# Moving the score step of the next mLSTM job ahead of the transposes of the present one, in a one-core decoder layer

## The reference, cut to what matters

```
s   = (q @ k^T) * exp(Dm - m_t)                    # scores of the chunk
num = w_inter * (q @ C) + s @ v                    # old state, and values
den = w_inter * (q . n) + sum(s)
h   = num / max(|den|, exp(-m_t))
C   = a_prev * C + (k * weight)^T @ v              # state carried to the next chunk
hn  = (h - mean(h)) * rsqrt(var(h) + eps) * g      # norm of each head
y_b = sigmoid(o) * hn
```

## Time and profile before

| | |
|---|---|
| median of 3 runs | 2973.88 us (2971.07 to 2974.53) |
| profiled execution, its own time | 2971.51 us |
| its span | 2969.8 us |
| PE busy | 2812.3 us, 95% |
| DVE busy | 1464.4 us, 49% |
| ACT busy | 865.9 us, 29% |
| POOL busy | 131.0 us, 4% |
| mean granted clock of TensorE | 0.973 |

### The profile page before, as it was taken

How to read it: one execution, slowest core, us unless ns; L and a number is a source line. 1 busy time by engine, 2 the same in 40 slices (tenths; PEclk the granted TensorE clock), 3 DMA queues, 4 the chain that set the end, 5 groups by cost and what they waited for, 6 DMA issues and landing times. The chain is left out here.

```text
span 2969.8 us, 44214 instructions
## 1 busy us (share of the span) xinstructions
PE 2812.3 (95%) x17401; PEld 2719.9 (92%) x17401; DVE 1464.4 (49%) x3023; ACT 865.9 (29%) x1396; POOL 131.0 (4%) x190
## 2 busy tenths in 40 slices
PE   5899999999999898999998998999899999999997
PEld 3799999999999888988988988998799999999996
DVE  4655455445443736436445534644764344343446
ACT  5422222222212422342333234234431111111114
POOL 2100000000002100000000000000200000000002
PEclk7899999999999999999999999999899999999998
DMA  7133223222210205212111220221111111111111
GB/s 232 44 99 99 97 87 99 88 96 79 76 43 15 58 25 152 72 43 77 54 61 33 88 71 29 91 72 43 50 43 43 42 42 42 42 42 42 42 43 61
DMA packets 168691, 197.48 MB, mean 66 GB/s; under 512 B 7896, under 2 KB 157172, under 8 KB 168517
## 3 DMA queue, kind: packets, MB, share of 16 engines
q1 hardware_dynamic: 168130, 195.62, 20.7%
q10 hardware_dynamic: 342, 0.15, 0.0%
q0 software_dynamic: 96, 0.00, 0.0%
HBM read 176.84 MB, written 18.91 MB: 66 GB/s over the span
## 5 line engine op out<-in xcount | busy, mean ns | idle before, releaser
L522 DVE SCALAR_TENSOR_TENSOR xT<-ps,gate_p,xT 128x384 f32<-128x384 f32 (+1 forms) x624 | 348.1, 570 | 116.3 <-PE ps L802 97.7
L908 PE MATMUL ps<-hhi,mw_hi 128*128 128x384 f32 (+1 forms) x1152 | 393.8, 342 | 8.7 <-DVE mw_lo L1702 7.6
L739 DVE TENSOR_TENSOR hf<-st,ps 128x384 f32<-128x384 f32 x132 | 70.2, 532 | 642.5 <-PE ps L823 640.4
L909 PE MATMUL ps<-hlo,mw_hi 128*128 128x384 f32 (+1 forms) x1152 | 381.3, 331 | 0.0
L910 PE MATMUL ps<-hhi,mw_lo 128*128 128x384 f32 (+1 forms) x1152 | 380.9, 331 | 0.0
L821 PE MATMUL ps<-hhi,wa_hi 128*128 128x384 f32 (+1 forms) x1056 | 350.2, 332 | 17.4 <-DVE wa_lo L729 14.5
L822 PE MATMUL ps<-hlo,wa_hi 128*128 128x384 f32 (+1 forms) x1056 | 347.9, 329 | 0.0
L823 PE MATMUL ps<-hhi,wa_lo 128*128 128x384 f32 (+1 forms) x1056 | 347.5, 329 | 0.0
L821 PE MATMUL ps<-hhi,wb_hi 128*128 128x384 f32 (+1 forms) x1056 | 346.1, 328 | 0.0
L823 PE MATMUL ps<-hhi,wb_lo 128*128 128x384 f32 (+1 forms) x1056 | 346.0, 328 | 0.0
L822 PE MATMUL ps<-hlo,wb_hi 128*128 128x384 f32 (+1 forms) x1056 | 345.9, 328 | 0.0
(11 more groups left out here) (296 smaller groups left out, 5087.1 us busy)
## 6 DMA issues: line engine op xcount, KB each, us to landing
ada_raw<-in_w_ada SPq DMA_DIRECT2D x36, 1024.0 KB, 5.1
mw_raw<-in_w_in SPq DMA_DIRECT2D x32, 1024.0 KB, 5.7
wa_raw<-in_w_ffn_in SPq DMA_DIRECT2D x22, 1024.0 KB, 5.1
wb_raw<-in_w_ffn_in SPq DMA_DIRECT2D x22, 1024.0 KB, 5.2
wo_raw<-in_w_ffn_out SPq DMA_DIRECT2D x22, 1024.0 KB, 5.0
ada_raw<-in_w_ada_final SPq DMA_DIRECT2D x8, 1024.0 KB, 5.5
cs<-in_state_mlstm_C SPq DMA_DIRECT2D x32, 256.0 KB, 5.5
out_C_sample<-cs SPq DMA_DIRECT2D x32, 256.0 KB, 2.4
```

What stands on the lines that cost most here:

```text
L522: ins = dve.scalar_tensor_tensor(out=xT[:, m, t0:t0 + wp], in0=ps[:, bank, 0:wp], scalar=gate_p[:, m:m + 1], in1=xT[:, m, t0:t0 + wp], op0 ...
L739: dve.tensor_tensor(M["hf"][:, n, 0:w], M["st"][:, n, 0:w], ps[:, up_bank("b", b, i, n), 0:w], ALU.mult).then_inc(C["hidden"].sem, 1)
L908: pe.matmul(out, wh, xh, start=(j == 0), stop=False)
L909: pe.matmul(out, wh, xl, start=False, stop=False)
```

## The change

The list of stages is put in another order, and the waits on PE follow it:

```diff
-            for gap in range(3 * NJ):
-                EVENTS.append(("stage", gap // 3, gap % 3))
+            stages = [(0, 0)]
+            for p in range(NJ):
+                stages += [(p, 1)] + [(p + 1, 0)] * (p + 1 < NJ) + [(p, 2)]
+            for gap, (p, stage) in enumerate(stages):
+                EVENTS.append(("stage", p, stage))
                 while unit < ((gap + 1) * 8 + 8) // 9:
@@ pair() of PE, in front of the matmuls of a pair
-                        pe.wait_ge(*K["st_done"](h * NJ + p + 1))
+                        pe.wait_ge(*K["st_done"](h * NJ + p + 2))
@@ stage0() of PE, in front of the transposes of k
-                            if p:
-                                pe.wait_ge(*K["h_kept"](h * NJ + p))
-                            else:
+                            if p > 1:
+                                pe.wait_ge(*K["h_kept"](h * NJ + p - 1))
+                            if p and place(p - 1)[0]:
+                                pe.wait_ge(*K["inter_done"](h * 8 + place(p - 1)[1] + 1))
+                            if not p:
                                 pe.wait_ge(*K["kw_done"](h * NJ + 1))
@@ in front of the scores
-                            if p <= PAIRS:
-                                pe.wait_ge(*K["seq_upd"](h * PAIRS + p))
+                            if 2 <= p <= PAIRS + 1:
+                                pe.wait_ge(*K["seq_upd"](h * PAIRS + p - 1))
@@ stage1() of PE
                             pe.wait_ge(*K["kw_done"](h * NJ + c + 2))
+                            if p:
+                                pe.wait_ge(*K["h_kept"](h * NJ + p))
@@ in front of scores times values
                             pe.wait_ge(*K["b5_read"](h * NJ + p))
+                            if p <= PAIRS:
+                                pe.wait_ge(*K["seq_upd"](h * PAIRS + p))
@@ stage2() of PE, in front of the transposes of num
                         if chunk:
                             pe.wait_ge(*K["inter_done"](h * 8 + c + 1))
+                        if p + 1 < NJ and place(p + 1)[0]:
+                            pe.wait_ge(*K["kw_done"](h * NJ + place(p + 1)[1] + 2))
                         else:
                             pe.wait_ge(*K["h_kept"](h * NJ + p))
```

## The result

The changed kernel takes 2948.43 us (median of 4 runs, 2947.67 to 2953.17), the kernel before 2974.19 us beside it. The ratio is 0.9919, with a 95% interval of 0.9902 to 0.9936: 25.8 us faster, where 20 were forecast (2954, range 2943 to 2966). The profiled execution took 2947.84 us, 23.7 less than the one of before. By the times alone the forecast's own stretch, 2949 to 2959, is missed by half a microsecond; the wider range holds it.

The account below looks back on a forecast made before the run. PE was taken to bound the kernel, busy 2812.3 of 2969.8 us, so only its waits could be won. Terms -16.3 + 5.1 - 1.4 - 7.4 = -20.0 us, clock 0, gave 2954 us, range 2943 to 2966.

Parts of the forecast that it names:

- (a): Stage 1 to stage 2 in jobs 0 to 7: a second unit removes DVE waits except job 8's, -16.3 us.
- (b): Job 2 to 3: scores' wait for the pair goes, new waits of 3.3 us a head come; +5.1 us.
- (c): Job 5 to 6: transposes of k stop waiting for ACT's copy, those of num wait for kw; -1.4 us.
- (d): End of the head: job 8's exponential moves before unit 21, so the last mix comes earlier; -7.4 us in all.
- (e): Pairs of jobs 0 and 1: scores ready in time with a margin of 0.35 us, cost 0.
- (f): Waits added on PE's queue: cost 0, between a loss of 2 us and nothing.
- (g): Clock: each stall pulls TensorE from 2.4 to 1.2 GHz for a while; net 0, between -8 and +12 us.
- rival 2: End of the head loses its clock penalty as stalls shrink: 3.5 us in two or more heads, 2946 us; chance 0.13.
- rival 1: One more slow spell of 1.75 us at job 2 and at job 8, all heads: 2964 us; chance 0.12.
- Rival 3: Exponential's table load stands behind its wait for DVE's exponent, scores 1.2 us later: 2966 us; chance 0.05.
- rival 4: PE stays at 1.2 GHz after job 2's stall for most of a job: 2981 us; chance 0.04.
- rival 5: An uncounted wait keeps stage 2 behind the scores' ACT work in every job: 2971 us, no change; chance 0.06.

Follow-up runs that it names:

- e5: The change for job 7 alone (job 8's stage 0 ahead of job 7's stage 2), against the kernel before: 2954.4 us, ratio 0.9919.
- e6: The change for jobs 0 to 6, job 8's stage 0 still behind job 7's stage 2, against the kernel before: 2964.8 us, ratio 0.9962.
- e7: The change for jobs 0 to 3 alone, the other jobs in the old order, against the kernel before: 2980.5 us, ratio 1.0016.
- e2: Kernel before with, in ACT's units from number 8 on, the wait for DVE's multiplication put ahead of that for PE's unit: 2964.62 us, ratio 0.9968.
- e3: Changed kernel with ACT's wait for DVE's multiplication put ahead of that for PE's unit, from unit 8 on: 2944.03 us, ratio 0.9897 to the kernel before.

## Why the prediction was right

**(a)**, second gap: predicted -16.3 us. All waits of L1984 for DVE outside job 8 are gone (24.7 to 1.7, all of it in job 8): right. e5, e6 and e7 show where it pays: jobs 4, 6 and 7, not jobs 0 to 3, whose one gap was enough. The second gap isn't all of it. In e7 job 4 keeps one gap and its 0.94 us goes all the same, since the unit's table load now stands ahead of its stage 1 (at 1285.58 in head 1); and e2, which only moves the load, takes 2.04 to 0.69. So some 1.35 us of each wait of 2.0 us at jobs 6 and 7 were the load's, and only the 0.7 left over needed the second gap.

**(b)**, job 2: 3.3 us a head predicted, 1.32 + 1.70 = 3.02 measured in heads 1 to 3 and 1.32 + 2.06 in head 4, together 12.4: +4.3 against +5.1. The idle column starts at the end of the last matmul's row, some 0.25 us after the next could start. By starts, as the prediction counted, the pair came 1266.44 - 1262.18 = 4.26 us after unit 7, where the work between takes 0.90: 3.36, the 3.3 predicted. In head 4 DVE took up the scores 0.46 us after ACT's exponential instead of 0.11; why isn't settled.

**(c)**, job 5: 3 x 0.45 + 0.37 = 1.7 instead of 2.4 us: -2.1 against -1.4.

**(d)**, the head's end: 17.08 to 15.58 us in heads 1 to 3, 17.16 to 14.22 in head 4: -7.4 as predicted. But the stretch now holds 0.32 us of transposes where it held 0.58 us of stage 0, and that work was only moved: 1.0 us too much was booked. (a) to (d) come to -20.5 measured, with that 1.0 taken off, and -20.0 predicted.

**(e), (f)**: no wait at the pairs of jobs 0 and 1, in head 1 or any other, though the margin was worked out as 0.35 us (in head 1's job 0 s_t ended at 1231.97 and the pair began at 1232.36, 0.39 later). No cost of the added waits is measurable: the rest rose by 1.3 us, and fell by 1.1 with the double count given back.

**(g)**, the clock, is the term that was mis-sized: 0 was put, -10.2 measured by the record of the clock, -7.9 without what ran beside stalls; -8 was the bound stated for it. Job 2's share was right in its sign, 13.7 us of low time to 23.9 (+5.1, predicted +3.5), and job 6's in size (-3.4, predicted -3.5). The heads' ends weren't taken to change, "the wait for mix_lo, 1.57, stays", and went from 27.3 us of low time to 3.4, nominally -11.9. The mix_lo wait did stay, at 1.45; what went was the 2.11 close ahead of it, down to 0.51. e5, which changes job 7 alone, frees three of the four ends as well, and e6, which leaves job 7 out, keeps 6.8 us at each. So rival 2 happened, larger than its 8 us, on top of part of rival 1's loss (a longer spell at job 2 in three heads, none behind job 8's new wait of 1.50). The measured 2948.4 is nearer to rival 2's 2946 than to the forecast's 2954. The forecast of the waits was right by its mechanism; that the clock's error stayed small enough for the range is luck in part, since +5.1 and -15.3 met in it. Some of this half time ran beside stalls, which is why stalls fell by 17.1 and not by 20.5: at the old ends of heads 2 to 4 a slow PE came late to the mix_lo wait and found it shorter (1.14, 0.65 and 1.06 us). By the table the whole is -17.1 of stalls, -10.2 of clock, +2.4 for what was counted in both, -1.1 of rest: -26.0 of 26.1 us.

Rival 3 would have shown as waits at jobs 0 and 1, rival 4 as a long spell behind job 2 (6.8 us was the longest), rival 5 as waits of L1995 in every job; none did. Nor did the estimate of 2968 come true: 0.02 us behind the load's end (1264.20 + 1.28) the exponential started, at 1265.50.

## What to carry to other kernels

When two kinds of work are interleaved, look where an interval is left empty: here it belonged behind the stage whose successor needs nothing fresh from the other engines, and that placement was worth more (28.6 us) than the reordering it served (25.8 us). Price a stall of TensorE at its length plus half of the low-clock spell that a trace shows behind it, and look at stalls that stand close together as one. A second interval for a chain pays only in the jobs whose first one was too short (and a good part of that shortage was the table load, by e2); in the others it was at best free here (e7: 1.0016).

## What the runs showed of the hardware that was not expected

- The activation table load takes a different place among two waits in a looped and in a written-out body. In the loop it ran late with PE's wait first and early with PE's wait second, in the last head the other way round (the earlier trace rows and the rows of e2; e3 does the same). That decides whether 1.28 us are hidden.
- Not each stall is followed by a spell at 1.2 GHz, as (g) put it. In the heads of these twelve traces, 11 lone waits of 1.50 to 1.55 us had none behind them, 5 of 8 of 1.67 us had one, and 18 of 28 of 1.93 to 2.10 us. The wait of 2.04 us at job 6 had none in head 1 before (1.00) and one in heads 2 and 3, with the same instructions around it.
- Two waits with less than 3 us of work between them: all 41 pairs that come to 2.6 us or more had a spell beside or behind them (3.4 us or longer), of 24 that come to about 2.0 us only 4.
